# First mixer of a two-block model: order of the first loads, the first weights in halves, first exponents before other work, two memsets on GpSimd, one copy earlier

## The reference, cut to what matters

```python
def hgrn2_recurrence(q, k, logf, v):          # 4 heads of 128, over chunks of tokens
    def step(S, xs):
        qc, kc, gc, vc = xs
        b = jnp.cumsum(gc, axis=2)
        o_inter = jnp.einsum('bhtk,bhkv->bhtv', qc * jnp.exp(b), S)
        diff = b[:, :, :, None, :] - b[:, :, None, :, :]
        decay = jnp.exp(jnp.where(causal[:, :, None], diff, -jnp.inf))
        scores = jnp.einsum('bhtsk,bhsk->bhts', qc[:, :, :, None, :] * decay, kc)
        ...

def hybrid_mixer(x, w_in, lower_bound, hgrn_norm_g, w_branch_sb, w_branch_hgrn, w_out):
    proj = x @ w_in                            # 256 x 1024 @ 1024 x 5632
    sq, sk, sv, hq, hf, hi, hg, gate_sb, gate_hg = jnp.split(proj, offsets, axis=-1)
    o_sb = stick_breaking_attention(heads(sq), heads(sk), heads(sv))
    f = lower_bound + (1.0 - lower_bound) * jax.nn.sigmoid(hf.astype(jnp.float32))
    o_hg = hgrn2_recurrence(silu(hq), 1.0 - f, log(f), hi)
    ...
    merged = jax.nn.sigmoid(gate_sb) * (o_sb @ w_branch_sb) + jax.nn.sigmoid(gate_hg) * (o_hg @ w_branch_hgrn)
    return merged @ w_out
```

## Time and profile before

| | |
|---|---|
| median of 3 runs | 1757.31 us (1755.16 to 1759.51) |
| the profiled execution, time | 1758.38 us |
| its span | 1756.6 us |
| PE busy | 1675.7 us (95%) |
| DVE / ACT / POOL busy | 689.2 / 578.2 / 72.1 us |
| read from HBM | 533.13 MB, 304 GB/s over the span |
| mean granted TensorE clock | 0.994 |

### The profile page before, as it was taken

The page is one execution under the profiler, slowest core; times in us unless marked ns, Lnnn a source line. Parts: engine busy times, 40 slices in busy tenths (PEclk is TensorE's granted clock), DMA queues, the critical chain, the costliest instruction groups (busy, mean ns, idle before and its releaser), DMA issues.

```text
span 1756.6 us, 24359 instructions
## 1 busy us (share of the span) xinstructions
PE 1675.7 (95%) x10063; PEld 1066.9 (61%) x10063; DVE 689.2 (39%) x1191; ACT 578.2 (33%) x818; POOL 72.1 (4%) x52
## 2 busy tenths in 40 slices
PE   6989999999999999999999999999999999999998
PEld 6989973333333333333333333338999898989996
DVE  3568662112212122121212121225498565657654
ACT  3743421101111111111111111125465577466433
POOL 2003100000000000000000000000110022000000
PEclk9999999999999999999999999999999999999999
DMA  8443389999999999999999999995565443555552
GB/s 258 144 137 121 128 366 426 411 416 423 431 429 431 429 431 429 431 430 431 429 431 430 431 430 431 430 371 165 171 189 170 144 144 124 170 176 191 171 197 87
DMA packets 150316, 535.04 MB, mean 305 GB/s; under 512 B 5548, under 2 KB 103988, under 8 KB 117489
## 3 DMA queue, kind: packets, MB, share of 16 engines
q1 hardware_dynamic: 149264, 532.11, 76.9%
q0 software_dynamic: 992, 2.10, 0.4%
HBM read 533.13 MB, written 1.05 MB: 304 GB/s over the span
## 4 chain that ended last, share of the span: by engine, by line
PE 55%; DMA 19%; ACT 2%; DVE 1%; issue 1%; SPq 0%; ACTq 0%
PE bank L1249 12%; DMA expert_weights_late<-in_expert_w_up_dram 10%; DMA expert_weights<-in_expert_w_up_dram 10%; PE bank L123 9%; PE bank L125 9%; PE bank L124 9%; PE bank L1265 7%; PE bank L1235 2%; PE bank L1216 2%; PE bank L1256 1%; ACT back_w_hi L107 1%; PE bank L1224 0%; PE bank L1840 0%; PE bank L1229 0%; ACT b_c_v L1553 0%
## 5 line engine op out<-in xcount | busy, mean ns | idle before, releaser
L1161 DVE TENSOR_TENSOR pre_act<-bank,bias_now 128x512 f32<-128x512 f32 x64 | 44.0, 688 | 673.1 <-PE bank L1256 673.1
L1249 PE MATMUL bank<-expert_weights_late,x_gathered 128*64 128x512 f32 x1024 | 227.4, 594 | 18.9 <-DMA expert_weights_late<-in_expert_w_up_dram 18.9
L111 DVE TENSOR_TENSOR back_w_lo<-raw_weights,back_w_hi 128x2048 fp32r<-128x2048 f32 x90 | 206.3, 2295 | 88.8 <-ACT back_w_hi L107 87.7
L107 ACT ACTIVATE back_w_hi<-raw_weights 128x2048 fp32r<-128x2048 f32 x90 | 170.2, 1892 | 97.9 <-PE bank L125 97.9
L123 PE MATMUL bank<-u_hi,back_w_hi 128*128 128x256 f32 x704 | 201.6, 286 | 0.2 <-DVE u_lo L1632 0.2
L124 PE MATMUL bank<-u_lo,back_w_hi 128*128 128x256 f32 x704 | 199.6, 284 | 0.0
L125 PE MATMUL bank<-u_hi,back_w_lo 128*128 128x256 f32 x704 | 199.5, 283 | 0.0
L1249 PE MATMUL bank<-expert_weights,x_gathered 128*64 128x512 f32 x768 | 170.9, 594 | 12.4 <-DMA expert_weights<-in_expert_w_up_dram 12.3
L1249 PEld LDWEIGHTS bank<-expert_weights_late,x_gathered 128*64 128x64 f32 x1024 | 71.7, 137 | 171.3 <-issue 132.2
L1093 ACT ACTIVATE up_rows<-bank 128x512 f32<-128x512 f32 x32 | 19.1, 597 | 415.3 <-PE bank L1249 415.3
L123 PEld LDWEIGHTS bank<-u_hi,back_w_hi 128*128 128x128 f32 x704 | 135.1, 192 | 2.4 <-issue 0.7
(11 more groups left out here) (403 smaller groups left out, 2750.4 us busy)
## 6 DMA issues: line engine op xcount, KB each, us to landing
expert_weights_late<-in_expert_w_up_dram SPq DMA_DIRECT2D x64, 2048.0 KB, 30.2
expert_weights<-in_expert_w_up_dram SPq DMA_DIRECT2D x48, 2048.0 KB, 30.2
expert_weights_late<-in_expert_w_down_dram SPq DMA_DIRECT2D x32, 2048.0 KB, 35.1
raw_weights<-in_w_in_dram SPq DMA_DIRECT2D x62, 1024.0 KB, 5.3
expert_weights<-in_expert_w_down_dram SPq DMA_DIRECT2D x24, 2048.0 KB, 35.1
raw_weights<-in_expert_w_up_dram SPq DMA_DIRECT2D x16, 2048.0 KB, 29.5
raw_weights<-in_w_up_dram SPq DMA_DIRECT2D x22, 1024.0 KB, 5.0
raw_weights<-in_expert_w_down_dram SPq DMA_DIRECT2D x8, 2048.0 KB, 34.6
```

The source lines that it names most:

```text
L107: act.activation(self.w_hi[:, s, 0:size], self.s.raw[:, s, 0:size], ACT.Copy).then_inc(self.hi_done, 1)
L111: dve.tensor_tensor(self.w_lo[:, s, 0:size], self.s.raw[:, s, 0:size], self.w_hi[:, s, 0:size].bitcast(FP32), ALU.subtract).then_inc(self. ...
L1161: dve.tensor_tensor(both.rearrange("p g k n -> p (g k) n").rearrange("p a (h n) -> p a h n", h=2), TB[b][:, :].rearrange("p (a h n) -> p a ...
L1249: m = pe.matmul(U[b][rows[half], :], lhsT=xg[:, 2 * u + a, :], rhs=w[:, a, 512 * c:512 * c + 512], start=(first and a == 0), stop=(last an ...
```

## The change

- SP loads the identity alone first, then the two token tiles as two DMAs with a semaphore each, then weight units 0 to 2, and only then the other six shared constants.
- GpSimd waits for weight unit 1 to land before its first DMA.
- PE's transposes run tile by tile, the first eight when tile 0 is there. The wait for all four `x_lo` is gone. gemm(0) is written out anew (`first_gemm`): all hi x hi, then all hi x x_lo, then all w_lo x hi, with waits for each piece; ACT and DVE split unit 0 in two halves of 1024 columns.
- DVE writes the exponents of level 0 right after the scans, before lo(14) and the two `sb_lo`.
- The memsets of Q and K go from DVE to GpSimd, behind `z_mm` 8 and `pv_mm` 2; DVE waits for both (`levels_zero`) before the first Q and K.
- ACT's copy of level(0)'s result stands before the `evac` of gemm(13), no longer behind it and hi(16).

The diff, without the semaphores' declarations:

```diff
         def sync(sp):
-            sp.dma_start(s.con[:, :, :], A["constants"][:, 0:len(SHARED) * P]...).then_inc(con_loaded, 16)
-            sp.dma_start(s.h[:, :, :], A["x"][0].rearrange("(a p) d -> p a d", p=P)).then_inc(x_loaded, 16)
+            sp.dma_start(s.con[:, 0, :], A["constants"][:, 0:P]).then_inc(identity_loaded, 16)
+            for t in range(TT):
+                sp.dma_start(s.h[:, t, :], A["x"][0, t * P:t * P + P, :]).then_inc(x_loaded[t], 16)
             for n, (seg, c) in enumerate(order):
                 st.load(sp, n // 3, n % 3, w_in[:, :, c0:c0 + COLS], KD, COLS)
+                if n == RING - 1:
+                    rest = A["constants"][:, P:len(SHARED) * P].rearrange("p (n c) -> p n c", c=P)
+                    sp.dma_start(s.con[:, 1:len(SHARED), :], rest).then_inc(con_loaded, 16)
...
         def gpsimd(pool):
             pool.memset(s.rows[:, :, :], 0.0).then_inc(rows_zero, 1)
+            pool.wait_ge(st.full[1], 16)
...
+            pool.wait_ge(z_mm, 8)
+            pool.memset(Q, 0.0).then_inc(levels_zero, 1)
+            pool.wait_ge(pv_mm, 2)
+            pool.memset(K, 0.0).then_inc(levels_zero, 1)
...
-            for n in range(RING):
+            act.wait_ge(st.full[0], 16)
+            for i in range(2):
+                act.activation(w_hi[:, 0, half_unit(i)], s.raw[:, 0, half_unit(i)], ACT.Copy).then_inc((first_hi, st.hi_done)[i], 1)
+            for n in range(1, RING):
                 split_hi(act, n)
...
-                evac(n, pair(hg, n - 12) if n < 14 else pair(gates, n - 14), ACT.Tanh, 0.5)
                 if j == 1:
                     act.wait_ge(lv_mm, 1)
                     act.activation(score[:, :, 1, :], s.bank[2][:, :]..., ACT.Copy).then_inc(cross_out, 1)
+                evac(n, pair(hg, n - 12) if n < 14 else pair(gates, n - 14), ACT.Tanh, 0.5)
...
-            for n in range(RING):
+            for i in range(2):
+                dve.wait_ge((first_hi, st.hi_done)[i], 1)
+                dve.tensor_tensor(w_lo[:, 0, half_unit(i)], s.raw[:, 0, half_unit(i)], w_hi[:, 0, half_unit(i)].bitcast(FP32),
+                                  ALU.subtract).then_inc((first_lo, st.lo_done)[i], 1)
+            for n in range(1, RING):
                 split_lo(dve, n)
...
-            split_lo(dve, 14)
-            for g in range(2):
-                low(pair(sb_lo, g), s.bank[6 + g][:, :], pair(sb_hi, g), (sb_hi_done, g + 1), sb_done)
-            dve.wait_ge(sb_done, 2)
-            step(dve.memset(Q, 0.0))
-            step(dve.memset(K, 0.0))
...
             exponent_args(0)
+            split_lo(dve, 14)
+            for g in range(2):
+                low(pair(sb_lo, g), s.bank[6 + g][:, :], pair(sb_hi, g), (sb_hi_done, g + 1), sb_done)
+            dve.wait_ge(levels_zero, 2)
...
         def tensor(pe):
-            pe.wait_ge(con_loaded, 16)
-            pe.wait_ge(x_loaded, 16)
-            for c in range(4):
-                for i in range(4):
-                    k, t = 2 * c + i // 2, i % 2
+            pe.wait_ge(identity_loaded, 16)
+            for t in range(TT):
+                pe.wait_ge(x_loaded[t], 16)
+                for k in range(KD):
+                    c, i = k // 2, 2 * (k % 2) + t
                     m = pe.transpose(s.bank[2 + c][:, P * i:P * i + P], s.h[:, t, k * P:k * P + P], C("identity"))
-                m.then_inc(tr_done, 1)
-            pe.wait_ge(tr_free, 4)
+                    if t == 1 and k % 2:
+                        m.then_inc(tr_done, 1)
...
+            def first_gemm():
+                hi, lo = st.w(0, KD, COLS)
+                for t in range(TT):
+                    c, out = slice(t * P, t * P + P), s.bank[0][:, T * t:T * t + T]
+                    for w, x in ((hi, x_hi), (hi, x_lo), (lo, x_hi)):
+                        for k in range(KD):
+                            if t == 0 and w is hi and x is x_hi:
+                                pe.wait_ge(tr_hi, k // 2 + 1)
+                                if k % 4 == 0:
+                                    pe.wait_ge((first_hi, st.hi_done)[k // 4], 1)
+                            if t == 0 and w is hi and x is x_lo:
+                                pe.wait_ge(tr_free, k // 2 + 1)
+                            if t == 0 and w is lo and k % 4 == 0:
+                                pe.wait_ge((first_lo, st.lo_done)[k // 4], 1)
+                            m = pe.matmul(out, lhsT=w[:, k, c], rhs=x[:, k, :], start=..., stop=...)
+                m.then_inc(st.gemm_done, 1)
...
-            for n in range(4):
+            first_gemm()
+            for n in range(1, 4):
                 gemm(n)
```

More of the change, by code:

```diff
@@ L267, in mixer1 @@
         evacuated = [sem(f"m1_evacuated{i}") for i in range(2)]
-        x_loaded, con_loaded, con1_loaded, small_loaded, ln_loaded = sem("x_loaded"), sem("con_loaded"), sem("con1_loaded"), sem("small_loaded"), sem("ln_loaded")
+        x_loaded, identity_loaded = [sem(f"x_tile{t}_loaded") for t in range(TT)], sem("identity_loaded")
+        first_hi, first_lo, levels_zero = sem("first_hi"), sem("first_lo"), sem("levels_zero")
+        con_loaded, con1_loaded, small_loaded, ln_loaded = sem("con_loaded"), sem("con1_loaded"), sem("small_loaded"), sem("ln_loaded")
         rows_zero, rows_loaded, cols_ready = sem("rows_zero"), sem("rows_loaded"), sem("cols_ready")
@@ L302, in wait_bank @@
                 pe.wait_ge(evacuated[b % 2], b // 2)
+        half_unit = lambda i: slice(i * KD * COLS // 2, (i + 1) * KD * COLS // 2)
         s.alpha_identity, s.gate_t, s.g_ready, s.first_h_ready = alpha_identity, gate_t, g_ready, h_ready
@@ L314, in sync @@
         def sync(sp):
-            sp.dma_start(s.con[:, :, :], A["constants"][:, 0:len(SHARED) * P].rearrange("p (n c) -> p n c", c=P)).then_inc(con_loaded, 16)
-            sp.dma_start(s.h[:, :, :], A["x"][0].rearrange("(a p) d -> p a d", p=P)).then_inc(x_loaded, 16)
+            sp.dma_start(s.con[:, 0, :], A["constants"][:, 0:P]).then_inc(identity_loaded, 16)
+            for t in range(TT):
+                sp.dma_start(s.h[:, t, :], A["x"][0, t * P:t * P + P, :]).then_inc(x_loaded[t], 16)
             w_in = A["w_in"][0].rearrange("(k p) n -> p k n", p=P)
@@ L505, in vector @@
             step(dve.memset(s.slot[:, :, PASSES * N_EXPERTS:], -1.0))
-            dve.wait_ge(con_loaded, 16)
+            dve.wait_ge(identity_loaded, 16)
             dve.tensor_scalar(alpha_identity[:, :], C("identity"), DEEPNORM_ALPHA, None, op0=ALU.mult).then_inc(alpha_ready, 1)
@@ L543, in vector @@
             dve.wait_ge(con1_loaded, 16)
+            dve.wait_ge(con_loaded, 16)
             softplus(0)
@@ L813, in tri_products @@
                     pe.wait_ge(con1_loaded, 16)
+                    pe.wait_ge(con_loaded, 16)
                 pe.wait_ge(sp_ready, g + 1)
@@ L837, in pv @@
                 m.then_inc(pv_mm, 1)
-            for n in range(4):
+            def first_gemm():
[12 more added lines that the diff above has]
+                                pe.wait_ge((first_lo, st.lo_done)[k // 4], 1)
+                            m = pe.matmul(out, lhsT=w[:, k, c], rhs=x[:, k, :], start=(w is hi and x is x_hi and k == 0), stop=(w is lo and k == KD - 1))
+                m.then_inc(st.gemm_done, 1)
+            first_gemm()
+            for n in range(1, 4):
                 gemm(n)
```

## The result

| | before | changed |
|---|---|---|
| median | 1756.57 us (4 runs, 1755.16 to 1759.51) | 1739.67 us (4 runs, 1738.65 to 1739.80) |
| ratio | | 0.990, 95% interval 0.9883 to 0.9918 |
| profiled execution, its span | 1758.38 us, 1756.6 us | 1739.80 us, 1737.9 us |
| first load of experts' weights | 224.81 us | 207.13 us |
| from there to the end of the span | 1531.8 us | 1530.8 us |

The account below looks back on a forecast made before the run. Outside four waits the mixer was taken as bound by PE's own work, the experts by their weight loads. Front 7.7 plus levels 8.7 gave 16.4 us off 1757.31: 1740.9, said as 1741, range 1737 to 1747.

Parts of the forecast that it names:

- What passes on: Mixer to experts: a microsecond saved before the first expert load at 224 us reaches the program's end in full.
- The start of gemm(0): First mixer matmul, released by half of hi(0): starts at 10.7 instead of 18.45 us, gaining 7.7 us.
- gemm(0)'s length: First mixer gemm: again 8.3 us, partly at low clock; 10.2 if all cold, 2.5 us gained if all warm.
- the front: Start of the mixer, loads through gemm(0): gain 7.7 us.
- The levels: PE at level(0) and level(1): waits of 2.48 and 3.06 us and twice 1.6 of low clock go, 8.7 us.
- Weight unit 3: Load beside GpSimd's DMAs: lands by 24.6 us, may land at 26.3, so costs nothing.
- The memsets: Q's and K's on GpSimd: K's may slow DVE by 0 to 2.2 us, at most 0.6 on the path; taken as 0.
- (a): Only part of the clock returns, or gemm(0) runs cold throughout: 11.3 us gained, 1746; chance 0.15 with milder mixtures.
- (b): One half does not pass on: DVE late at level(0), 1745, or weight unit 3 late, up to 1749; chance 0.08.
- (c): GpSimd's memsets and DVE block each other in full: 0.6 us on the path, 1741.5; inside the forecast's 0.72.
- (d): GpSimd's small loads land after DVE's need at 41 us, each microsecond on the path; at 65 us 1765; chance 0.02.
- (e): DMAs taken in another order, tile 0 landing with tile 1 and unit 0: front gains 5.5, 1743; inside 0.72.

Follow-up runs that it names:

- e4: Changed kernel plus matmuls nobody reads on PE, 5 before the transposes and 5 between them and gemm(0): 1737.97 us.
- g1: Changed kernel without GpSimd's wait for weight unit 1 before its first DMA: 1744.37 us.
- e3: e1 with 5 and 7 matmuls nobody reads ahead of level(0) and level(1), keeping PE busy during the waits: 1745.88 us.
- g3: Changed kernel with the other six constants (384 KB) loaded ahead of the token tiles: 1741.12 us.
- e1: Changed kernel with the levels as before (exponents behind lo(14) and sb_lo, memsets on DVE, ACT's copy behind gemm(13)'s output): 1746.97 us.
- f1: Changed kernel with ACT's copy of level(0)'s result back behind the output of gemm(13) and hi(16): 1745.45 us.
- f2: Changed kernel with both memsets on DVE again, behind sb_lo, exponents still first: 1739.89 us.
- f3: Changed kernel with the exponents of level 0 behind lo(14) and sb_lo again, memsets still on GpSimd: 1740.91 us.
- e2: Kernel before with only the levels part of the change (exponents first, memsets on GpSimd, ACT's copy moved): 1749.16 us.
- g2: Changed kernel with GpSimd's loads held back until lo(6) is done: 1741.33 us.

## Why the prediction was right

Measured 1739.67 against 1741 forecast, inside 1737 to 1747.

- **What passes on.** Right: in all fourteen traces the span from the first expert load to the end lies between 1528.8 and 1531.8 us, while that load itself moves from 207 to 225. The mixer's microseconds reach the end one for one, to within those 3 us.
- **The start of gemm(0).** Forecast 10.7, measured 10.73. That the number is met to the hundredth is luck in part. Tile 0 was 0.5 us later than said (5.18 for 4.7), ACT's four copies made that up (hi(0) begins 1.93 us after the first of them, the forecast had 2.5), and the first half of hi(0) with its hand-over took 1.2 where 1.0 was reckoned. That ACT and not unit 0 sets the start holds by almost nothing. The forecast had unit 0 at 9.0 and ACT at 9.7; e4 shows unit 0 at 9.46, and ACT came at 9.51. Without GpSimd's wait it does not hold at all, as g1 shows.
- **gemm(0)'s length** was taken as 8.3 us, the value of before, with 5.8 and 10.2 as the ends. It was 7.3 (10.73 to 18.21, less the hand-over of 0.2) in this trace and 7.8 in the second of the same kernel; reckoned alike it was 8.5 in e3 and 8.4 in g3. So 8.3 is a possible value, and this execution was luckier than the forecast: this is the term that was mis-sized, by up to 1 us. In the traces the first expert load moved 17.7 us and not 16.4: the front gave 8.7 instead of 7.7, the levels 9.0 instead of 8.7. The medians show 16.9. That the time itself lies 1.3 below the 1741 comes from 0.5 of this and from the median of the kernel before, which stood at 1757.31 when the forecast was made and at 1756.57 with its fourth run.
- **The levels.** Forecast 8.7, measured 9.0. Both waits went, and in this pair of traces also both falls of the clock (granted clock 1.00 from 100 to 134 us). But the 3.2 us for the clock are not a fixed price: e1 paid 1.5 of it with both waits in place, f1 1.4. The forecast's sum took one execution's luck for the rule.
- **Weight unit 3** landed at 22.3, inside the bound of 24.6; no matmul waited for it. GpSimd's first DMA went out at 12.74, forecast at 12.
- **The memsets** cost the path nothing. Beside GpSimd's memset of K DVE's copy into E takes 0.61 or 0.62 us in all nine traces where the two meet, and 0.41 or 0.42 in the five where they don't (before, e1, e3, f2, f3; in f2 the copy stands in the same place and only the memset is gone). So it is 0.2 us, within the forecast's bound of 0 to 2.2, but not the nothing that "a memset reads nothing" stood for. The rule of the Trainium skill (GPSIMD Engine Reference, section 1, Specifications) names DVE instructions with two SBUF inputs and those in a 2-port performance mode. Beside a memset the first half is not seen: the subtraction, with two inputs, took 0.69 beside it and 0.69 in f2 without it; the one that lost is the copy. Beside GpSimd's addition the same half agrees, with the product that took 2.89 us instead of 0.68.
- **The rivals.** (a) and (b) did not occur; that thin router matmuls lower the clock is refuted by e2. (c) would have cost up to 0.6 us and cost none. (d) was mis-sized: it set the deadline at 41 us and one microsecond for each beyond it. g2 brought DVE's data at 48.9, almost 8 us behind that deadline, and PE lost 1.4 us, since DVE had 5 us of waiting behind that line to give. (e) did not occur.

## What to carry to other kernels

A load that nobody needs soon still takes its share of the DMA engines from one that everybody waits for: holding GpSimd's 1.4 MB back by one semaphore was worth 4.8 us of the 16.9; splitting the first weights in halves showed nothing. Look at what stands ahead of a short copy in an in-order queue: one ACT copy moved ahead of two instructions gave 4.5 us in the trace and 5.9 in the median. Removing short idle stretches of PE brings the wait and sometimes the clock behind it, so for waits of 2.5 to 3 us like these, price the clock as a range, from nothing to 1.6 us each.

## What was not expected of the hardware

- The same idle time of PE did not always have the same consequence. After 3.06 us of it level(1) took 3.53 and 3.36 us (before, f1) or 2.02 (e1), where the full clock gives 1.95.
- A clock once up can fall again behind a gap of about 2 us while matmuls are already running: in e4 and in the second trace of the changed kernel the first matmuls of gemm(0) ran fast and later ones slowly. In that second trace (granted clock 0.85 from 11 to 12 us, 0.50 from 12 to 15):

```profile
10.84 0.71 PE L874 MATMUL bank<-x_hi,m_w_hi 128*128 128x256 f32 x4 [2.24 <-ACT m_w_hi L394]
11.79 1.19 PE L874 MATMUL bank<-x_hi,m_w_hi 128*128 128x256 f32 x4 [0.24 <-ACT m_w_hi L394]
12.78 1.91 PE L874 MATMUL bank<-x_lo,m_w_hi 128*128 128x256 f32 x8
```

- The kernel before scatters over 7 us, the changed one over 1.3, and the cause was not found. The two idle stretches with their sometimes low clock could give or take 1.6 us each, so 3.2 of the 7. The runs do not bear it out: e1 has both waits and scatters over 2.7 us, e2 has neither and scatters over 2.5, and the mean granted clock of the single executions of the kernel before does not go with their times (1754.56 us at 0.993, 1758.17 at 0.996).
